# A two-layer hybrid decoder with experts on one core: sums of squares between full products, expert routing by ordered values, and slot products, overflow table and last outputs in other places

## The reference, cut to what matters

```python
u = rms_norm(x, norm_mix) @ w_in                 # columns of groups A, B, C, D
yA = mla_mixer(uA); yB = pool_mixer(uB); yC = swa_mixer(uC); yD = conv_mixer(uD)
x = x + concat(rms_norm(y) for y in (yA, yB, yC, yD)) @ w_mix_out
x = x + cross_attention(rms_norm(x), rms_norm(mem), ...)
t = rms_norm(x)
g_idx = argmax(t @ w_group + b_group)            # the best of 4 groups
e_prob = softmax((t @ w_expert + b_expert)[rows, g_idx])
top_p, top_i = top_k(e_prob, 2)                  # the best 2 of its 8 experts
y[e] = (silu(t @ w_gate[e]) * (t @ w_up[e])) @ w_down[e]
x = x + sum over the 2 experts of weight * y[e]
```

## Time and profile before

| | |
|---|---|
| runs of the kernel | 1198.85 us median of 3 (1197.72 to 1200.7) |
| the profiled execution | 1202.07 us, of which the trace's span is 1200.3 us |
| granted TensorE clock, mean over the span | 0.97 |
| TensorE busy with products | 1133.7 us (94%) |
| VectorE busy | 693.8 us (58%) |
| ScalarE busy | 367.5 us (31%) |
| read from HBM | 240.19 MB |

### The profile page before, as it was taken

How to read it: one execution, slowest core, us unless ns; L and a number is a source line. 1 busy time by engine, 2 the same in 40 slices (tenths; PEclk the granted TensorE clock), 3 DMA queues, 4 the chain that set the end, 5 groups by cost and what they waited for, 6 DMA issues and landing times.

```text
span 1200.3 us, 16831 instructions
## 1 busy us (share of the span) xinstructions
PE 1133.7 (94%) x4956; PEld 618.5 (52%) x4956; DVE 693.8 (58%) x1637; ACT 367.5 (31%) x799; POOL 45.3 (4%) x87
## 2 busy tenths in 40 slices
PE   7999999999879999999889998999996899999996
PEld 3854556456664444444457545555564644444443
DVE  4345574457676555555752475544676855555556
ACT  4216231023433333333242262211143423333331
POOL 8000000000006000000000000000000000000000
PEclk9999998999989999999999999989997999999999
DMA  9130023410228999999641300245005189999991
GB/s 284 51 123 18 1 70 108 165 80 1 89 122 292 411 422 421 422 422 422 241 149 40 101 1 1 71 140 210 1 1 210 58 360 404 422 422 422 422 420 78
DMA packets 53453, 243.04 MB, mean 202 GB/s; under 512 B 8976, under 2 KB 19504, under 8 KB 28048
## 3 DMA queue, kind: packets, MB, share of 16 engines
q1 hardware_dynamic: 49760, 240.40, 50.6%
q0 software_dynamic: 2528, 1.89, 0.8%
q10 hardware_dynamic: 1104, 0.02, 0.1%
HBM read 240.19 MB, written 2.10 MB: 202 GB/s over the span
## 4 chain that ended last, share of the span: by engine, by line
PE 81%; DVE 10%; issue 3%; ACT 2%; DVEq 2%; DMA 1%; ACTq 1%; SPq 0%
PE ps L2634 17%; PE ps L2200 11%; PE ps L2444 9%; PE ps L2656 9%; PE ps L2192 7%; PE ps L2599 5%; PE ps L2170 5%; PE ps L2600 4%; PE ps L2492 2%; PE ps L2224 2%; PE ps L2280 2%; DMA X<-in_x 1%; PE ps L2288 1%; PE ps L2311 1%; PE ps L2499 1%
## 5 line engine op out<-in xcount | busy, mean ns | idle before, releaser
L2634 PE MATMUL ps<-wgu,xw 128*64 128x512 f32 x1024 | 225.3, 592 | 0.0
L2035 DVE TENSOR_TENSOR X<-ps,X 128x512 f32<-128x512 f32 x256 | 156.5, 681 | 10.3 <-issue 6.1
L2200 PE MATMUL ps<-hT,ring 128*128 128x512 f32 x352 | 157.6, 603 | 0.0
L2634 PEld LDWEIGHTS ps<-wgu,xw 128*64 128x64 f32 x1024 | 73.1, 137 | 144.7 <-issue 143.6
L2656 PE MATMUL ps<-wdn,hhT 128*64 128x512 f32 x512 | 118.6, 606 | 3.2 <-ACTq L1233 3.2
L2444 PE MATMUL ps<-ring,yT 128*128 128x512 f32 x256 | 119.3, 616 | 0.3 <-DVE X L1402 0.3
L856 ACT ACTIVATE xw<-xgT 128x512 f32 (+1 forms) x132 | 81.9, 624 | 106.2 <-issue 92.4
L2599 PE MATMUL ps<-yhi,Wt 128*128 128x512 f32 x256 | 107.2, 419 | 4.1 <-DVEq L1288 3.5
L2200 PEld LDWEIGHTS ps<-hT,ring 128*128 128x128 f32 x352 | 67.1, 195 | 77.6 <-issue 77.6
L2600 PE MATMUL ps<-ylo,Wt 128*128 128x512 f32 x256 | 100.9, 394 | 0.0
L2058 DVE SCALAR_TENSOR_TENSOR ylo<-ps,ws,yhi 128x512 fp32r<-128x512 f32 x64 | 48.0, 750 | 63.5 <-ACTq L1250 61.5
(11 more groups left out here) (374 smaller groups left out, 1374.4 us busy)
## 6 DMA issues: line engine op xcount, KB each, us to landing
wgu<-in_w_gate SPq DMA_DIRECT2D x64, 1024.0 KB, 11.7
wgu<-in_w_up SPq DMA_DIRECT2D x64, 1024.0 KB, 13.7
wdn<-in_w_down SPq DMA_DIRECT2D x64, 1024.0 KB, 14.0
ring<-in_w_in SPq DMA_DIRECT2D x8, 1024.0 KB, 6.6
ring<-in_w_mix_out SPq DMA_DIRECT2D x12, 512.0 KB, 6.3
w_kv<-in_xa_w_kv SPq DMA_DIRECT2D x4, 1024.0 KB, 9.5
ring<-in_w_in SPq DMA_DIRECT2D x2, 2048.0 KB, 17.8
ring<-in_w_in SPq DMA_DIRECT2D x2, 1536.0 KB, 16.6
```

The lines of the kernel that those rows point to most:

```text
L2035: tt(xh, bank, xh, ALU.add).then_inc(mfreed((what, n)), 1)
L2200: last = mm(bank, w[:, c, c0:c0 + P], hT[:, c, :], start=c == 0, stop=c == KD - 1)
L2634: last = mm(bank[r], xw[:, c, j, 0:SLOTS], wgu[2 * parity + j][:, :, c, :], start=c == 0, stop=c == KD - 1)
```

## The change

1. **Sums of squares.** Group A's 12 sums go between the first products of ("B", 0): 6 behind the first, 6 behind the second. At n = 7 only the 8 `sqS` sums are left. At n = 8 each of the 8 products of ("D", 5) is followed by one `sqP` sum, and 8 of the sums of ("stY", 1) come behind them; 6 are left at n = 9. VectorE copies ("stY", 0) at n = 8.
2. **Routing.** The two rounds of maximum, mark and push down become 4 MAX (the 8 largest values in order, for one token tile), 4 MAX_INDEX (their places), and one comparison of 256 elements with the places.
3. **Step 0.** VectorE runs `tiles_past` before the second half of `sorted_gain`, and makes `diag` before `hh` (place_ready); `ranked` comes behind `hh` with a signal of its own, ranked_ready. TensorE does the places' products before the transposes of `hh`, and the slots' weights before the down products.
4. **Overflow table.** Two of its three sums of tiles go into step 0 before `spread`, the rest behind step 0's `ylo`; step 15 has none. VectorE and ScalarE read the registers before step 15.
5. **Last outputs.** The last 8 products come in the order 0, 2, 4, 6 (left halves, as soon as the first `ylo` is there), then 1, 3, 5, 7; VectorE adds in that order.

The core of the diff, with four spaces for sixteen of indentation:

```diff
         step_(2 * i + 2, 0, True)
-    step_(PAIRS - 1, 1, False)
     wait_apart(act, S["route_ready"], l + 2)
...
     before = act.value_load(ovf[0:1, 1:2], min_val=0, max_val=DEPTH * OVF)
+    step_(PAIRS - 1, 1, False)
...
     dve.drain()
-    nc.vector.tensor_reduce(r1(6), experts, AX_X, ALU.max)
+    for t in range(NT):
+        nc.vector.max(best[:, t], experts[:, t])
     dve.drain()
-    first_of(experts, NE, rf(6), rf(15), r32(10))
-    is_first(r32(7), rf(15), NE, ALU.is_equal)
-    stt(experts, r32(7), -2.0 * BIG, experts, ALU.mult, ALU.add)
+    for t in range(NT):
+        nc.vector.max_index(found[:, t], best[:, t], experts[:, t])
     dve.drain()
-    nc.vector.tensor_reduce(r1(9), experts, AX_X, ALU.max)
+    shape = [P, 2, NT, NE]
+    tt(rt[:, 7:9].rearrange("p k (t e) -> p k t e", t=NT),
+       iota[:, 0:NE].unsqueeze(1).unsqueeze(1).to_broadcast(shape),
+       found[:, :, 0:2].rearrange("p t k -> p k t").unsqueeze(3).to_broadcast(shape), ALU.is_equal)
     dve.drain()
-    first_of(experts, NE, rf(9), rf(15), r32(10))
-    is_first(r32(8), rf(15), NE, ALU.is_equal)
     tt(M16[:], r32(7), r32(8), ALU.add)
     signal("M_ready")
-    tt(rf(11), rf(9), rf(6), ALU.subtract)
+    tt(rf(11), best[:, :, 1], best[:, :, 0], ALU.subtract)
...
+    def tile_sums(dst, of):
...
+        tt(passed, begun[:], of.unsqueeze(1).to_broadcast([P, OVF, NE]), ALU.mult)
+        dve.drain()
+        nc.vector.tensor_reduce(dst.unsqueeze(2), passed, AX_X, ALU.add)
+        dve.drain()
...
     def overflow_table():
...
-        for dst, of in ((first, first_from), (second, second_from), (split, split_from)):
-            tt(passed, begun[:], of.unsqueeze(1).to_broadcast([P, OVF, NE]), ALU.mult)
-            dve.drain()
-            nc.vector.tensor_reduce(dst.unsqueeze(2), passed, AX_X, ALU.add)
...
+        nc.vector.tensor_copy(slot[:], slot_0[:])
+        signal("place_ready")
...
+    def ranks_shown():
...
         for j in range(2):
...
                flat(rank_k).unsqueeze(2).to_broadcast(shape), ALU.is_equal)
-        nc.vector.memset(all_ones, 1.0)
-        nc.vector.tensor_copy(slot[:], slot_0[:])
-        signal("place_ready")
+        signal("ranked_ready")
...
             spread(parity)
-        if isinstance(p, int) and p == PAIRS - 1:
-            overflow_table()
         dve.wait_ge(S["silu_ready"], mdone(l, p, "silu_ready", 1))
...
         else:
-            placed()
+            ranks_shown()
             signal("params_free")
...
             slot_weights()
+            tile_sums(first, first_from)
+            tile_sums(second, second_from)
+            dve.wait_ge(S["places_ready"], done(l, "places_ready", 2))
             spread(parity)
...
             signal("ylo_ready")
+        if not back:
+            overflow_table()
...
+    tiles_past()
     sorted_gain(1)
-    tiles_past()
     padded_places()
+    placed()
+    chosen(rank_k, rank)
     token_weights()
...
             step_(2 * i + 1 + k, 1 - k, True)
-    step_(PAIRS - 1, 1, True)
-    dve.drain()
     n_ovf = dve.value_load(ovf[0:1, 0:1], min_val=0, max_val=OVF - 1)
     before = dve.value_load(ovf[0:1, 1:2], min_val=0, max_val=DEPTH * OVF)
+    step_(PAIRS - 1, 1, True)
+    bring_back(PAIRS - 1, "last comb", LAST_ORDER[0:NT])
     for t in range(NT):
-        bring_back(PAIRS - 1, "last comb", (2 * t, 2 * t + 1))
+        bring_back(PAIRS - 1, "last comb", LAST_ORDER[NT + t:NT + t + 1])
         signal("x_final")
...
-            def channels(l, name, w, c0):
+            def channels(l, name, w, c0, beside=None):
...
     bank = bank_of(l, name)
+    other = bank_of(l, beside[0]) if beside and beside[0] else None
     for c in range(KD):
         last = mm(bank, w[:, c, c0:c0 + P], hT[:, c, :], start=c == 0, stop=c == KD - 1)
-    last.then_inc(filled(name), 1)
+        if c == KD - 1:
+            last.then_inc(filled(name), 1)
+        if beside:
+            beside[1](other, c)
...
-    for t in range(NT):
-        q = slice(t * P, (t + 1) * P)
-        mm(bank[:, 2 * t:2 * t + 1], sqA[:, 0, q], ones[:, 0:1], start=True, stop=False)
-        mm(bank[:, 2 * t:2 * t + 1], sqA[:, 1, q], ones[:, 0:1], start=False, stop=True)
-        last = mm(bank[:, 2 * t + 1:2 * t + 2], sqA[:, 2, q], ones[:, 0:1], start=True, stop=True)
-    last.then_inc(filled(("stA",)), 1)
     ring1_wait(pe, l, 4)
-    channels(l, ("B", 0), ring1, 0)
...
+    def latent_sums(bank, c):
...
+        for t in range(2 * c, min(2 * c + 2, NT)):
+            q = slice(t * P, (t + 1) * P)
+            mm(bank[:, 2 * t:2 * t + 1], sqA[:, 0, q], ones[:, 0:1], start=True, stop=False)
+            mm(bank[:, 2 * t:2 * t + 1], sqA[:, 1, q], ones[:, 0:1], start=False, stop=True)
+            last = mm(bank[:, 2 * t + 1:2 * t + 2], sqA[:, 2, q], ones[:, 0:1], start=True, stop=True)
+            if t == NT - 1:
+                last.then_inc(filled(("stA",)), 1)
+    channels(l, ("B", 0), ring1, 0, (("stA",), latent_sums))
...
             channels(l, ("D", 4), ring0, P)
-            pe.wait_ge(S["sqP_ready"], done(l, "sqP_ready", 2))
             pe.wait_ge(S["sqO_ready"], done(l, "sqO_ready", NT))
...
             for k in range(2):
-                sums(bank, NT * k, sqP[:, k], range(NT))
+                sums(bank, 8 + NT * k, sqS[:, k], range(NT))
+        if n == 8:
+            pe.wait_ge(S["sqP_ready"], done(l, "sqP_ready", 2))
+            pooled_bank = ps[:, dense.job["stY", 0][0], :]
...
+            def pooled_sums(_, c):
+                last = sums(pooled_bank, c, sqP[:, c // NT], [c % NT])
+                if c == KD - 1:
+                    last.then_inc(filled(("stY", 0)), 1)
+            channels(l, ("D", 5), ring0, GW + P, (None, pooled_sums))
+            pe.wait_ge(S["sqC_ready"], done(l, "sqC_ready", 1))
+            pe.wait_ge(S["sqO_ready"], done(l, "sqO_ready", NT + 2))
+            bank = bank_of(l, ("stY", 1))
+            sums(bank, 0, sqC_[:, 0], range(NT))
             for k in range(2):
-                last = sums(bank, 8 + NT * k, sqS[:, k], range(NT))
-            last.then_inc(filled(("stY", 0)), 1)
-        if n == 8:
-            channels(l, ("D", 5), ring0, GW + P)
+                sums(bank, 8 + 3 * k, sqM[:, k], range(2))
         if n == 9:
...
             pe.wait_ge(S["sqO_ready"], done(l, "sqO_ready", 2 * NT - 1))
-            bank = bank_of(l, ("stY", 1))
+            bank = ps[:, dense.job["stY", 1][0], :]
+            sums(bank, NT, sqC_[:, 1], range(NT))
             for k in range(2):
-                sums(bank, NT * k, sqC_[:, k], range(NT))
-            for k in range(2):
-                last = sums(bank, 8 + 3 * k, sqM[:, k], range(3))
+                last = sums(bank, 10 + 3 * k, sqM[:, k], [2])
             last.then_inc(filled(("stY", 1)), 1)
...
+    def slot_places():
...
                ).then_inc(mfilled(("places", k)), 1)
...
+    def slot_weights():
...
+        pe.wait_ge(S["ranked_ready"], done(l, "ranked_ready", 1))
...
             bring_back(p, "comb", range(5), 1 - parity)
+        else:
+            slot_places()
         pe.wait_ge(S["hh_ready"], mdone(l, p, "hh_ready", 1))
...
             bring_back(p, "comb", range(5, 8), 1 - parity)
+        else:
+            slot_weights()
         for j in range(2):
...
     step_(0, 0, False)
-    slots()
     with pe.Fori(0, PAIRS // 2 - 1) as i:
...
     before = pe.value_load(ovf[0:1, 1:2], min_val=0, max_val=DEPTH * OVF)
-    pe.wait_ge(S["ylo_ready"], mdone(l, PAIRS, "ylo_ready", 0))
     pe.wait_ge(S["Wt_ready"], mdone(l, PAIRS, "Wt_ready", 0))
-    bring_back(PAIRS - 1, "last comb", range(8), 1)
+    for h in range(2):
+        pe.wait_ge(S["ylo_ready"], mdone(l, PAIRS - 1, "ylo_ready", h + 1))
+        bring_back(PAIRS - 1, "last comb", LAST_ORDER[h * NT:(h + 1) * NT], 1)```

How it moves instructions. TensorE around n = 7 to 9 of the dense part, before (PT, vA are the attention's output products, kTA, qTA its scores, Pr the transposes of its weights, mask rows add the mask):

```order
L2200 MATMUL ps<-hT,ring_94 128x512 x8
L2288 MATMUL ps<-ones,sqP 128x1 x8
L2288 MATMUL ps<-ones,sqS 128x1 x8
L2280 MATMUL ps<-PT,vA 64x128 x6
...
L2170 MATMUL ps<-ident,Pr 128x128 x6
L2200 MATMUL ps<-hT,ring_94 128x512 x8
L2280 MATMUL ps<-PT,vA 64x128 x6
...
L2170 MATMUL ps<-ident,Pr 128x128 x8
L2288 MATMUL ps<-ones,sqC__66 128x1 x8
L2288 MATMUL ps<-ones,sqM 128x1 x6
L2444 MATMUL ps<-ring_95,yT 128x512 x6
```

28 lines of the change are left out of this document (15 added, 13 removed).

## The result

| | before | with the change |
|---|---|---|
| median of the runs | 1198.28 us of 4 (1197.35 to 1200.7) | 1184.76 us of 4 (1182.45 to 1190.26) |
| ratio of the times | | 0.989 (95%: 0.9869 to 0.9912) |
| the profiled execution | 1202.07 us, span 1200.3 | 1183.12 us, span 1181.3 |
| mean granted TensorE clock | 0.97 | 0.98 |

The kernel is 13.5 us faster. The time lies inside the range (1169 to 1188), but the forecast of 1175.5 was 9 us too low, and 1184.76 is also above the forecast's own upper bound of 1181: it is inside only because the range takes in the clock rival, at 1185.7.

What follows compares the result with a forecast made beforehand. TensorE works 94% of the span, so time comes from pauses, half-clock products and products that need not stand alone. Terms 10.2 + 1.3 + 3.0 + 3.0 + 4.0 + 1.6 + 0.2 = 23.3 us give 1175.5 us; range 1169 to 1188.

Steps and rivals of the forecast that it cites:

- the clock rival: The clock does not follow the sums, or falls only move; the 10.2 us stay, 1185.7 us; chance 14%.
- Clock behind the sums, 10.2 us: ("B", 0) and n = 7 to 9: spreading sums ends half-clock losses of 11.3 us, one half left; bounds 0 and 11.3.
- list of pauses: Four TensorE pauses named in each layer: the routing, step 0, step 15 and the last additions.
- The sums' own time, 1.3 us: Sums alone behind full products hide part of their 0.22 us load: 0.08 saved each, 16 sums; bounds 0 and 0.11.
- Routing, 3.0 us: VectorE's MAX and MAX_INDEX at 0.25 us each: 2.7 us instead of 4.17, 1.5 gained in each layer.
- Step 0, 3.0 us: Moved slot products; step 1 delayed 1.4 us (bounds 0.5 and 2.2); 0.25 kept in layer 1, 2.8 in layer 2.
- Step 15, 4.0 us: Without the overflow table ahead of hh, the last down products come 2.0 us sooner in each layer.
- Last outputs, 1.6 + 0.2 us: Layer 1's last additions start 1.6 us earlier without register reads; layer 2's end gains 0.2 (bounds -0.5 and 1.5).
- The mixed stretches: Rival: sums behind full products count as weak, ("B", 0) and ("D", 5) at half clock, 1214.6 us; chance 4%.

Runs made afterwards that it cites:

- b0_bank4: The changed kernel with ("B", 0) in PSUM bank 4 instead of bank 2; median 1180.67 us, 0.9834 of before.
- routing_back: The changed kernel with the two old routing rounds in place of MAX, MAX_INDEX and the comparison; median 1190.75 us, 0.9936 of before.
- table_later: b0_bank4 with the overflow table in four pieces between spread and hh of steps 1 to 4, none in step 0; median 1173.82 us, 0.9818 of before.
- last_mixed: b0_bank4 with the last outputs in the order 0, 2, 1, 3, 4, 5, 6, 7; median 1175.42 us, 0.9805 of before.
- keys_first: combined, with VectorE copying the turned keys ahead of the convolution at n = 3; median 1165.48 us, 0.9727 of before.
- keys_sumsY: keys_first with the sums of n = 7 to 9 together again (16 at n = 7, 14 at n = 9); median 1175.02 us, 0.9816 of before.
- all_spread: b0_bank4 with group A's sums three behind each of four products, n = 7 and 8 sums one or two behind each product; median 1177.73 us.
- sumsY_together: The changed kernel with the sums of n = 7 to 9 put back as before the change; median 1193.74 us, 0.9945 of before.
- combined: b0_bank4, all_spread, table_later and last_mixed in one kernel; median 1172.56 us, 0.9791 of before.
- slots_back: table_later with step 0's slot products back behind its down products and diag back behind hh; median 1179.2 us, 0.9839 of before.

## Why the forecast was right and wrong

**Clock behind the sums, 10.2 us: the step that failed.** At n = 7 to 9 it held in this trace, and more than held: the stretches from the first scores to the last output product are 13.6 us shorter, 3.4 of it two falls behind the wait at n = 3 (at 136 and 726 us) that did not come in this run. That was luck. In its list of pauses the prediction also missed the one at n = 3; the chain of before has it, and half clock follows at 135.9:

```profile
132.67 2.27 issue
```

Nor is the gain at n = 7 to 9 sure: no stretch was to hold more than 8 sums, but at n = 8 nine stand in a row, and 3 of 16 layers with this order have a fall there. The failure is ("B", 0). I had it at full clock with its sums spread, and asked of the sums only what they do to the clock. That they also covered a wait, for PSUM bank 2, I did not see, since no row of before shows a wait there. It cost 3.7 us of waiting and 3.8 us more, 3.4 of them in layer 1 as half clock (10.2 us in place of 3.4). Net 6.1 us gained in place of 11.5 (with the next term). b0_bank4 gives the 3.7 back with one number.

**The sums' own time, 1.3 us: nothing.** A pair of one full product and one sum takes 1.08 us (769.85 to 770.93 in b0_bank4), a full product 0.86: the sum costs 0.22 behind a full product as it does in a row. The lower bound was right.

**Routing, 3.0 us: 4.6.** The mechanism was right and the two prices too high: 0.12 us for a MAX and 0.18 for a MAX_INDEX (0.74 for four), not 0.25 each. The trace agrees with the Trainium skill (Vector Engine (DVE) Microarchitecture Reference, "The match/index hardware and the swap-based sort pattern") that the position needs a load and a search, 0.07 and 0.18 us; but the load is cheaper than the 0.19 us that I had for each pass. In layer 2 the stretch shrank by 1.2 us more, by luck: before, half clock began at 914.1 us, inside the last products of the logits, which took 3.14 us, and with the change behind them (1.95 us). routing_back, with the old rounds, takes 1.95 too.

```profile
913.63 3.14 PE L2499 MATMUL ps<-w_rt,hT 128*128 128x36 f32 x16 [0.38 <-ACT lg L856]
...
902.68 1.95 PE L2532 MATMUL ps<-w_rt,hT 128*128 128x36 f32 x16 [0.38 <-ACT lg L860]
```

**Step 0, 3.0 us: 2.6.** Both slot products and the transposes in the order counted; the down products began 11.43 us behind `gu` (1.2 forecast later, 1.35 and 1.1 measured). The delay of step 1 was 2.2 and 2.0, my upper bound, and not 1.4: `hh` came 2.6 us behind its silu (375.51 to 378.12), where I had counted 1.9. In layer 2 the half clock went. In layer 1 0.2 us were kept (0.25 forecast): table_later shows that the weights would have taken the rest anyway.

**Step 15, 4.0 us: 4.0.** Down products 14.58 us apart again.

**Last outputs, 1.6 + 0.2 us: 1.2 + 0.2.** The additions began 1.2 us nearer to `ylo`. At the end of layer 2 the 1.3 us gained went into the stores, as forecast; last_mixed shows that this was the order's price.

**The rivals.** The clock rival was half right. The Trainium skill (TensorE: Matmul & The Clock Gate, "HAM oscillation — how this bites in real kernels") ties falls to waits; the fall at n = 3, which keys_first removed, agrees with it, though the page's example has waits of some 3 to 5 us and this one is 2.3. keys_sumsY, with falls behind sums and no wait, shows that it isn't the whole rule. The mixed stretches with one, two or three sums behind a full product are not weak (all_spread). Without its part at n = 7 to 9 the change is 9 us slower by the medians (sumsY_together, 12 runs), and keys_first 9.5.

**The forecast's time.** 4.3 of the 9 us are the terms above (23.3 forecast, 19.0 between the profiled executions; the stretches make 19.9, of which 0.6 is lost ahead of the first mark). Of the 19.0, 4.6 are draws of the clock and no work of the change: the two falls at n = 3 and the logits of layer 2. Of the others, 3.2 are by how much the profiled execution of before stood above its median, which I took off, and 1.6 by how much the changed kernel's stood below its own. I had read the losses from one trace, slower than any of the 35 other runs of before, and treated the falls in it as fixed places with a price; they are draws, and a kernel that keeps a wait of 2.3 us and weak stretches keeps their spread.

## What to carry to other kernels

Before moving work off a place, ask what it covers there as well as what it costs: a block of cheap instructions may be the only cover of the PSUM bank that the next one needs, and the profile of before shows no wait there. Where TensorE's clock falls, list all its weak stretches, one-column streams and waits alike, and remove them together: each run punishes some of them, so removing one shows little, and with the last gone the five runs agreed within 1.3 us. And look where the freed time can go: in layer 1 the weights took back all 2.2 us that step 1 had gained (table_later), in layer 2 nothing did.

## What the runs showed of the hardware that I had not expected

- On 128 partitions a MAX of 32 elements takes 0.12 us, the load of its 8 values 0.07 to 0.09, the search of 32 elements 0.18, and four pairs of load and search together 0.74; a 4-element TENSOR_TENSOR takes 0.17.
- A one-column product costs TensorE 0.22 us whether it stands in a row (3.47 us for 16) or between full products (1.08 us for the pair, 0.86 for the full one).
- The same order of instructions got half clock in one layer and full clock in the other (keys_sumsY: 755.7 us in layer 2, nothing in layer 1), and from run to run.
- Two sums behind each full product kept the granted clock at 1.00 (all_spread, combined and keys_first, n = 8), while six behind each of two products did not always (layer 1 of b0_bank4, 89.9 to 93.3 us, and of last_mixed; full clock in table_later and slots_back).
